# Turning the gathered expert rows: VectorE in 32x32 pieces in place of TensorE

## What is computed

```python
def step(acc, blk):
    e, tok, wt = blk
    xb = h[tok]
    hb = jax.nn.silu(xb @ we_g[e]) * (xb @ we_u[e]) 
    return acc.at[tok].add(wt[:, None] * (hb @ we_d[e]).astype(jnp.float32)), None
shared = (jax.nn.silu(h @ ws_g) * (h @ ws_u)) @ ws_d
```

## Time and profile before

| | us |
|---|---|
| median of 3 runs | 1125.21 (1124.67 to 1125.6) |
| the profiled execution | 1126.64 |
| its span, first to last instruction | 1124.8 |
| TensorE busy, VectorE busy | 1094.1, 462.7 |
| ScalarE busy, GpSimd busy | 236.4, 135.3 |
| DMA: bytes moved, mean rate | 337.16 MB, 300 GB/s |

### The profile page before, as it was taken

The page is one execution under the profiler, slowest core; times in us unless marked ns, Lnnn a source line. Parts: engine busy times, 40 slices in busy tenths (PEclk is TensorE's granted clock), DMA queues, the critical chain, the costliest instruction groups (busy, mean ns, idle before and its releaser), DMA issues.

```text
span 1124.8 us, 16922 instructions
## 1 busy us (share of the span) xinstructions
PE 1094.1 (97%) x6443; PEld 575.1 (51%) x6443; DVE 462.7 (41%) x1286; ACT 236.4 (21%) x516; POOL 135.3 (12%) x163
## 2 busy tenths in 40 slices
PE   6999999999999999999999999999999999999896
PEld 3456677777877545754343443443444444343232
DVE  2218541565456645843274233233232232331157
ACT  4131241222133123211111111111111111111111
POOL 0210000000020010121112112111111121121100
PEclk9999999999999999999999999999999999999999
DMA  9857622021170273899999999999999999999598
GB/s 370 326 207 295 227 79 75 1 85 51 62 266 7 103 255 120 311 365 426 423 425 426 424 417 425 425 416 396 421 409 384 426 399 400 417 391 370 209 412 344
DMA packets 51655, 337.16 MB, mean 300 GB/s; under 512 B 9637, under 2 KB 14089, under 8 KB 30831
## 3 DMA queue, kind: packets, MB, share of 16 engines
q1 hardware_dynamic: 33710, 287.32, 63.0%
q0 software_dynamic: 17856, 48.68, 11.8%
HBM read 311.30 MB, written 37.24 MB: 310 GB/s over the span
## 4 chain that ended last, share of the span: by engine, by line
PE 91%; DMA 4%; DVE 2%; ACT 1%; issue 1%; SPq 0%; DVEq 0%; POOLq 0%; ACTq 0%
PE bank L1561 30%; PE bank L1584 15%; PE bank L1257 10%; PE bank L1276 5%; PE bank L1549 4%; DMA mem<-expert_out_rows 3%; PE bank L1375 3%; PE bank L1376 3%; PE bank L1170 3%; PE bank L1493 3%; PE bank L1254 3%; PE bank L1145 1%; PE bank L1572 1%; PE bank L1340 1%; PE bank L1154 1%; PE bank L1128 1%
## 5 line engine op out<-in xcount | busy, mean ns | idle before, releaser
L1561 PE MATMUL bank<-mem 128*32 128x512 f32 (+2 forms) x1488 | 304.5, 594 | 0.6 <-DVE mem L2247 0.6
L1561 PEld LDWEIGHTS bank<-mem 128*32 128x32 f32 (+2 forms) x1488 | 100.6, 126 | 166.0 <-issue 166.0
L1584 PE MATMUL bank<-mem 128*32 128x512 f32 (+2 forms) x744 | 157.0, 596 | 0.1
L2247 DVE COPY mem<-bank 128x512 f32<-128x512 f32 x48 | 33.2, 691 | 283.3 <-PE bank L1549 283.3
L1257 PE MATMUL bank<-hT,mem 128*128 128x288 f32 x512 | 133.3, 410 | 1.0 <-ACT mem L935 1.0
L1257 PEld LDWEIGHTS bank<-hT,mem 128*128 128x128 f32 x512 | 93.9, 190 | 25.7 <-issue 2.4
L1561 PE MATMUL bank<-x_sb,mem 128*32 128x512 f32 (+2 forms) x416 | 99.3, 594 | 0.0
L1065 ACT ACTIVATE mem<-bank 128x256 f32<-128x256 f32 x48 | 18.4, 384 | 313.0 <-PE bank L1572 312.8
L1584 PEld LDWEIGHTS bank<-mem 128*32 128x32 f32 (+2 forms) x744 | 48.7, 126 | 61.4 <-issue 60.6
L2262 DVE COPY hT<-bank 128x512 f32<-128x512 f32 x48 | 33.2, 691 | 85.7 <-PE bank L1584 85.6
L790 POOL DMA_INDIRECT mem<-ffn_in_rows,idxg x32 | 32.9, 1028 | 264.5 <-DVE idxs L2243 211.0
(11 more groups left out here) (400 smaller groups left out, 1281.2 us busy)
## 6 DMA issues: line engine op xcount, KB each, us to landing
mem<-k_w_exp SPq DMA_DIRECT2D x51, 2048.0 KB, 23.3
mem<-in_w_exp_down SPq DMA_DIRECT2D x51, 1024.0 KB, 22.7
x_sb<-k_w_exp SPq DMA_DIRECT2D x13, 2048.0 KB, 21.4
mem<-k_w_ada SPq DMA_DIRECT2D x8, 2048.0 KB, 9.0
mem<-k_w_in SPq DMA_DIRECT2D x7, 2048.0 KB, 9.7
hT<-in_w_exp_down SPq DMA_DIRECT2D x13, 1024.0 KB, 25.4
mem<-expert_out_rows SPq DMA_DIRECT2D x6, 2048.0 KB, 16.5
mem<-k_w_head SPq DMA_DIRECT2D x4, 2048.0 KB, 18.4
```

The source lines that it names most:

```text
L1561: i = mm(bank[sl, :], xT[:, j % 2, c * BLK + sl.start:c * BLK + sl.stop], wview(r)[0][:, c, :], start=c == 0, stop=c == KC - 1)
L1584: i = mm(ps[4 + hf][sl, :], hhT[:, k * BLK + sl.start:k * BLK + sl.stop], wview(r)[1][:, k, hf * 512:(hf + 1) * 512], start=k == 0, stop=k ...
```

## The change

`x_T`, its waits and the two PSUM copies go for all blocks but block 0, which is turned by TensorE and copied by ScalarE and VectorE as before. In the place of VectorE's copy stands `turn`, 16 STREAM_TRANSPOSE instructions: each reads 32 partitions (slots) of `xg`, and of each of the eight chunks 32 neighbouring values, and writes them as 32 partitions of `xT`, so that a pair (q, a) of source and destination partition groups covers the piece of all eight chunks. The turn waits for the gather itself and, from block 2 on, for the up products of the block two before (`eup`), which read the same half of `xT`. One semaphore `xT_ready` replaces `xgT_a`, `xgT_d` and, for GpSimd's reuse of the gather buffers, `xgT_t`. SyncE's waits are renamed alike.

```diff
-            def xT_evac(n, j):
-                dve.wait_ge(S["xgT_t"], n + 1)
-                cp(xT[:, j % 2, 4 * BLK:8 * BLK], ps[1][:, :]).then_inc(S["xgT_d"], 1)
+            def turn(n, j, s=None):
+                g = gbuf(n, j)
+                dve.wait_ge(S[f"gat{g}"], gcount(n, j, s))
+                if not (isinstance(n, int) and n < 2):
+                    dve.wait_ge(S["eup"], n - 1)
+                rows = xg[g].rearrange("s (c d) -> s c d", c=KC)
+                cols = xT[:, j % 2, :].rearrange("d (c s) -> d c s", c=KC)
+                for q in range(P // QS):
+                    for a in range(P // QS):
+                        sl, dl = slice(q * QS, (q + 1) * QS), slice(a * QS, (a + 1) * QS)
+                        i = dve.transpose(cols[dl, :, sl], rows[sl, :, dl])
+                i.then_inc(S["xT_ready"], 1)
...
             def up(n, j, parts, cs=range(KC)):
-                pe.wait_ge(S["xgT_a"], n + 1)
-                pe.wait_ge(S["xgT_d"], n + 1)
+                if isinstance(n, int) and n == 0:
+                    pe.wait_ge(S["x0T_a"], 1)
+                pe.wait_ge(S["xT_ready"], n + 1)
...
                 elif n >= XG:
-                    pool.wait_ge(S["xgT_t"], n - XG + 1)
+                    pool.wait_ge(S["xT_ready"], n - XG + 1)
```

More of the change, by code:

```diff
@@ L645, in _ @@
             sp.wait_ge(S["eup"], max(LASTB[r] for r in range(NE) if slot(r) == XSLOT) + 1)
-            sp.wait_ge(S["xgT_t"], NBK)
+            sp.wait_ge(S["xT_ready"], NBK)
             for t in range(NT):
@@ L666, in _ @@
             overflow(sp, nov, body, last=last_rows)
-            sp.wait_ge(S["xgT_a"], NBK)
-            sp.wait_ge(S["xgT_d"], NBK)
+            sp.wait_ge(S["xT_ready"], NBK)
             for k in range(2):
@@ L1080, in _ @@
                 shared_silu(i)
-            xT_evac(0, 0)
+            act.wait_ge(S["x0T_t"], 1)
+            a(xT[:, 0, 0:4 * BLK], ps[0][:, :], ACT.Copy).then_inc(S["x0T_a"], 1)
             shared_silu(NSH - 1)
@@ L1093, in _ @@
             out_rows(NBK - 1, NBK - 1)
-            overflow(act, nov, body, lambda: xT_evac(NBK, NBK))
+            overflow(act, nov, body)
             for i, (t, _) in enumerate(COMBINE):
@@ L1537, in find_idx, with first_x_T @@
                 i.then_inc(S["idx_mm"], 1)
[L1539 to L1547, removed]
+            def first_x_T():
+                pe.wait_ge(S["gat0"], gcount(0, 0))
+                pe.wait_ge(S["sh_ready"], NSH - 1)
                 for c in range(KC):
-                    i = tr(ps[c // 4][:, (c % 4) * BLK:(c % 4 + 1) * BLK], xg[g][:, c * P:(c + 1) * P], ident[:, :])
-                i.then_inc(S["xgT_t"], 1)
+                    i = tr(ps[c // 4][:, (c % 4) * BLK:(c % 4 + 1) * BLK], xg[0][:, c * P:(c + 1) * P], ident[:, :])
+                i.then_inc(S["x0T_t"], 1)
             def up(n, j, parts, cs=range(KC)):
-                pe.wait_ge(S["xgT_a"], n + 1)
-                pe.wait_ge(S["xgT_d"], n + 1)
+                if isinstance(n, int) and n == 0:
+                    pe.wait_ge(S["x0T_a"], 1)
+                pe.wait_ge(S["xT_ready"], n + 1)
                 if not (isinstance(n, int) and n < 2):
@@ L1616, in _ @@
             shared_up(KC // 2)
-            x_T(0, 0)
+            first_x_T()
             shared_up(2)
@@ L1661, in _ @@
             overflow(pe, nov, body, first_blocks, last_done)
-            for name in ("xgT_a", "xgT_d", "ehh", "ehT", "eout_a", "eout_d", "idx_ready"):
+            for name in ("xT_ready", "ehh", "ehT", "eout_a", "eout_d", "idx_ready"):
                 pe.wait_ge(S[name], NBK)
@@ L2266, in body @@
                 gated(n, j)
-                xT_evac(n + 1, j + 1)
+                turn(n + 1, j + 1, s + 1)
                 idx_out(n + 2, j + 2, s + 2)
@@ L2280, in _ @@
             place(2)
-            xT_evac(0, 0)
+            dve.wait_ge(S["x0T_t"], 1)
+            cp(xT[:, 0, 4 * BLK:8 * BLK], ps[1][:, :]).then_inc(S["xT_ready"], 1)
             shared_mul(NSH - 1)
@@ L2287, in _ @@
                 if b < NBK - 1:
-                    xT_evac(b + 1, b + 1)
+                    turn(b + 1, b + 1)
                 gated(b, b)
@@ L2302, in first_blocks @@
                 place_more(NBK + 1, NBK + 1, 1)
-                xT_evac(NBK, NBK)
+                turn(NBK, 0, 0)
                 idx_out(NBK + 1, NBK + 1)
```

20 lines of the change are left out of this document (4 added, 16 removed).

## The result

The changed kernel takes 1132.6 us (median of 4 runs, 1132.1 to 1133.4) against 1125.4 for the kernel before on the same chip: ratio 1.0065, 95% interval 1.0048 to 1.0083, so 7.2 us slower. The forecast was 1129.9, or 4.7 slower. The profiled execution spans 1130.6 us (before 1124.8).

A forecast was written before the change was run, and what follows sets the result against it. TensorE's instruction stream was taken as the bound, the weight stream right under it. TensorE's saving -16.4, start +5.3, tables +12.4 and clock +3.4 gave +4.7 us: 1129.9 us against the median 1125.21, range 1118 to 1165.

The forecast's parts named there:

- jams: Places where TensorE waits for VectorE: block 1, +5.3 us, and blocks 8 to 10 behind the tables, +12.4 us.
- TensorE's saving: Transposes gone from TensorE, down products then waiting for ScalarE's copy: -16.4 us over 46 blocks.
- start: Block 1: TensorE's up products wait for VectorE's turn after the gather, +5.3 us.
- tables and clock: VectorE's overflow tables of blocks 6 to 8 delay later turns, +12.4 us; two half-clock stretches after TensorE idles, +3.4 us.
- The turn: VectorE's 16 transpositions per block, without overlap, 0.45 us each, 7.2 us together, hidden in the steady beat.
- Rival B: VectorE becomes the bound in every block if a transposition costs above 0.53 us: 1165 or 1252 us; chance 0.24.
- the 0.21 between the copy and the down products: Each block: down products follow ScalarE's copy of the hidden rows by 0.21 us, as at the last block.
- The weights don't bind: At block 21 TensorE would be 13 us later than before, so weight loads cost nothing.
- rival C: The weight stream caps the gain at about 9 us, 1116 us; chance 0.29 together with the rival of overlapping transpositions.
- Gathers late: Sign that the forecast is wrong altogether: gathers, issued later, land after VectorE wants them; about 3 us to spare.

The follow-up runs named there:

- light loads: Half the gate/up bytes left out from the sixth expert on: kernel before 1126.1 us, changed kernel 1127.4, changed kernel with both jams removed 1105.9, without a turn 1105.4.
- experiment 6: Changed kernel with its 16 transpositions kept, but each square left in its own group of 32 partitions: 1132.1 us, ratio 1.0060.
- experiment 1: Changed kernel with block 1 turned by TensorE and the overflow tables spread over blocks 6 to 24: 1130.7 us, ratio 1.0048.
- experiments 1, 3 and 4: 1: see experiment 1. 3: changed kernel without transpositions, 1124.5 us. 4: instead 16 one-value copies, 1129.8, 32 copies, 1137.4, or four 128-partition transpositions, 1125.7; kernel before plus 16 copies, 1130.5.

## Why the prediction was right, and where its steps were not

The forecast, 4.7 slower, has the right sign and is 2.5 us off. The mechanism was right in part: jams at two places against a shorter beat. That the sum came so near is in part luck, since a wait of 5.85 us that it put at nothing was made up for by a saving that was 3 larger and by jams that were 2 cheaper.

| term, us | forecast | full loads, from the trace |
|---|---|---|
| TensorE's saving | -16.4 | -19.5 |
| start | +5.3 | +5.4 |
| tables and clock | +12.4, +3.4 | +13.8 |
| waits for weights | 0 | +5.85 |
| sum | +4.7 | +5.5 |

The deficit at block 47 is 6.1, and the spans differ by 5.8; the saving is that of the light loads.

- *The turn*, 0.45 each and 7.2: 0.449 and 7.18. Right. The hold that the Trainium skill states in "VectorE: DVE Perf Modes", "Two Vector instructions with no wait between them" is now shown by experiment 6. Rival B is out.
- *The start*, +5.3: 5.4.
- *Tables and clock*, +12.4 and +3.4: too high by 2. The deficit rises by 10.1 from block 7 to block 10 and by 2.0 from block 1 to block 2, and in these four beats 1.7 was saved besides, hence 13.8. The prediction had the stalls at 2.8, 5.8 and 3.7. TensorE's timeline shows 2.55 at block 8, 0.83 and 3.39 at block 9, and 1.11 at block 10:

```profile
587.58 8.77 PE L1549 MATMUL bank<-mem 128*32 128x512 f32 x64 [2.55 <-issue]
...
597.55 0.28 PE L1528 MATMUL bank<-mem 128*128 128x7 bf16 x5 [0.83 <-DVE mem L2188]
...
619.24 3.21 PE L1549 MATMUL bank<-mem 128*32 128x512 f32 x28 [1.11 <-issue]
```

  The sum added clock to stalls, but while TensorE worked at half clock (3.4 us each at blocks 8 and 9, 1.7 lost each) VectorE went on at its own pace, so that the next stalls were shorter than forecast, by 1.6 and 2.6. At block 1 the stretch at half clock was 10.2 long and not 3.4, 5.0 of it with TensorE at work.
- *TensorE's saving*, -16.4: mis-sized. The step that failed is the 0.21 between the copy and the down products, read from the last block, where TensorE had stood idle for 1.08 before. In the steady beat it is 0.14 in the mean and TensorE's idle about 0.3. The gap of 0.56 less 0.14 is 0.42 a beat, so a beat is 11.50 (light loads), not 11.58, and 46 beats save 19.5.
- *"The weights don't bind"*: wrong, and the largest error, 5.85 us. I looked at block 21, where TensorE was indeed late enough, and not at blocks 40, 46 and 47, by when it had won back all but 3 us. My price for the cap was wrong too. I let rival C gain up to 9 us; without any turn the gain was 0.5 (ratio 0.9996). I took the DMA's free share behind 743.4 for room. The marks speak against that: in the last load of the kernel before, the changed one, the one without a turn and experiment 1, the twelfth mark stands 3 to 8 us ahead of the thirteenth. So I read the free share as that of engines with nothing to do while the slowest work.
- *What nobody had in the ledger*: 16 VectorE instructions a block make each load's last sixteenth late. In the changed kernel that lag is 3.0 and not 8.0. I hold that the jams mask it: during them the DMA ran dry (113.3 MB moved from 455 to 740, against 117.3 before and 117.3 in experiment 1), so that the engine behind caught up and all four slow ones were late together; the last load's marks are 1048.5, 1049.8, 1050.1 and 1051.1. Experiment 6, with smaller jams, lies between in both: 115.8 MB and a lag of 7.5. That would be why removing the jams gave 1.9 of some 20: the late sixteenth held the loads back to 1050.2 by itself. This last step is argued from the marks; experiments 1, 3 and 4 show its two halves.
- *Gathers late*: none was. TensorE's waits for VectorE stand at blocks 1 and 8 to 10 only, as foretold.

Neither repair pays: the hold, the jams and the turn itself could all go, and the kernel would stand where it stood (0.9996). No version faster than both was found.

## What to carry to other kernels

When one engine and a weight stream are nearly equal limits, follow the spare time of every load to the end, with the gain you expect added up; a block that is late enough in the middle says nothing of the last one. Count VectorE's instructions as well as their time: where the DMA is full, more of them can make the weights late, as 752 one-value copies did here. What sets a load's landing is the slowest of its sixteen parts, which neither GB/s nor the mean share shows. To learn what an engine's saving is worth, halve the other limit and measure the pair.

## What the runs showed of the hardware that I had not expected

Idle VectorE time isn't free: 752 copies of one value, on an engine 41% busy, cost 4.3 us. Of the 8 KB packets of kind "instruction", 1457 added instructions bring 12, 705 bring 5 and 752 in the kernel before bring 4, so one for 120 to 190. A second queue of that kind, which I take for TensorE's, has packets of 16 KB, 54 before and 51 after 376 products with their weight loads were taken out, so one for about 250. The Trainium skill, "Advanced Engine Details and Errata", "ISA Cache", gives one line size, 16 KB or 256 instructions, and no other for any engine: the trace agrees where TensorE's instructions went, and shows packets of half that size, and fewer instructions to each, where VectorE's were added.

A transposition of 128 partitions x 256 float32 values took 412 ns and one of 32 partitions 436, so three quarters of the lanes stood unused in the change's turn. With an idle of TensorE of 7.0 us came 10.2 us at a granted clock of 0.50, half of them still in the idle; behind idles of 2.55 and 3.39 us came 3.4 us each.
